# Eight trains of identity-by-ones products on TensorE, placed ahead of waits in four stages of a two-block model

## The chip, the cores and the metric

The kernel runs on one core of a Trainium2 chip. The metric is the device time of one execution in microseconds (us); lower is better. A core has five engines with instruction queues of their own, each worked through in order: TensorE (matmuls; PE in the profile), VectorE (DVE), ScalarE (ACT), GpSimd (POOL) and SyncE (SP, which here only issues transfers). Engines wait for one another by semaphores. TensorE's clock is granted by the chip at one of two levels, 1.2 and 2.4 GHz; the profile gives it as a share, 0.50 and 1.00.

## The reference

1024 tokens of width 1024 go through two blocks in float32. The first: a mixer (long convolutions and Fourier transforms), then a mixture of 32 experts in 4 groups. Each token chooses a group and two experts in it:

```python
g_sel = jnp.argmax(g_logits, axis=-1)
top_l, top_i = lax.top_k(e_logits, TOP_K)
expert = (g_sel[:, None] * EXPERTS_PER_GROUP + top_i)
...
y = (jax.nn.silu(xb @ w_gate[e]) * (xb @ w_up[e])) @ w_down[e]
```

The second block:

```python
proj = rms_norm(x) @ w_in                  # q, k, v, u, gates
mix = (g_a * y_a + g_b * y_b) @ w_o        # chunked attention and pooling, gated
x = x + rms_norm(mix)
x = x + rms_norm(conv_gated_ffn(rms_norm(x)))   # up projection to 2 x 2816, conv, gated GELU, down projection
```

## The kernel before

The stages run one after the other. Each is a block of instructions for all engines: it begins when all engines have come out of the one before, and ends when all have finished their part. Most matmuls are products of split float32 numbers, three matmuls each (`product`, lines 141 to 143). `m.ident` and `m.ones` are 128x128 float32 matrices in the on-chip memory; `keep_clock` (line 146) is defined and never called. As a measure of a plain float32 matmul: `channel_transform` (line 726) issues 32 of 128x128 by 128x128 in one train, each with weights of its own.

**The routing** (`route`, line 1379). VectorE works out from the logits which expert each token goes to, in a chain of small instructions. Twice it needs TensorE: `pairs_done` lets two matmuls go that rank the tokens (`route_ps`, lines 1446 and 1448), `rank_mm` gives them back; after `places_done` 16 matmuls build the list of rows (line 1455), `list_mm` gives it back. From the list come the row numbers (`ids_done`), and GpSimd gathers the first three blocks' rows with them (line 1375). SyncE loads the first expert weights in the meantime (line 1342) until all raw slots are full, and goes on only in the next block, `experts`, whose first work on TensorE is to transpose a block's rows (line 1644).

**The second projection's begin** (`project_second`, line 1986). For each of eight tiles of 128 tokens VectorE adds up the two expert rows and the residual and scales it twice, TensorE transposes it (line 2143, eight transposes), ScalarE and VectorE split the result into `hT`. A tile goes on when VectorE has scaled it (`scaled_done`). From tile 4 on, half a product of 24 matmuls follows the transposes. `row_done` is given once, early, when ScalarE has read a row out of the first PSUM bank.

**The end of `mix_output`** (line 2764). For each of eight tiles: 48 matmuls (`tile_product`), then the transposes of the tile before (`turn`, line 2813). The last tile's transposes stand alone, after the loop. VectorE then brings them out and mixes them with other tiles (lines 2865 to 2880), and the block ends.

**The up projection** (`ffn_up`, line 2965). ScalarE and VectorE split seven blocks of the input (`blocks_high`, `blocks_rest`) and the operands (`up_operand_high`, `up_operand_rest`). TensorE's n-th group of matmuls waits for `rest_done`.

Of the kernel before, what the change touches and what calls it, by code (L numbers as in the profile page):

```python
# [17 lines left out]
F32 = mybir.dt.float32  # L18
# [127 lines left out]
def keep_clock(nc, m, out, n):  # L146


    for _ in range(n):
        nc.tensor.matmul(out, m.ident[:], m.ones[:], start=True, stop=True)  # L150
# [1228 lines left out]
def route(nc, m, A, router, weights, rows):  # L1379
# [3 lines left out]
    with ExitStack() as mem:  # L1383
# [58 lines left out]
        @block.tensor  # L1442
        def _(pe):

            pe.wait_ge(pairs_done, 1)
            nc.tensor.matmul(ps[:, 1, 0:(TT + 1) * EXPERTS], m.ones[:], earlier[:].rearrange("p t e -> p (t e)"),
                             start=True, stop=False)
            last = nc.tensor.matmul(ps[:, 1, 0:TT * EXPERTS], before[:], both[:].rearrange("p t e -> p (t e)"),
                                    start=False, stop=True)
            last.then_inc(rank_mm, 1)  # L1450

            pe.wait_ge(places_done, 1)
            for slot in range(2):
                for t in range(TT):
                    last = nc.tensor.matmul(ps[0:CAP, 0, 0:BLOCKS], at_row[:, slot, t, :], in_block[:, slot, t, :],
                                            start=(slot == 0 and t == 0), stop=(slot == 1 and t == TT - 1))
            last.then_inc(list_mm, 1)

        @block.gpsimd
        def _(pool):  # L1460
# [511 lines left out]
def mixture(nc, m, A):  # L1972

    with ExitStack() as mem:
        m.row_ids = mem.enter_context(nc.sbuf_tensor("row_ids", [CAP, BLOCKS], I32))
        m.out_ids = mem.enter_context(nc.sbuf_tensor("out_ids", [CAP, BLOCKS], I32))
        with ExitStack() as places:
            weights = ExpertWeights(nc, m, places, A)
            weights.add_parts(nc, places)
            rows = Rows(nc, m, places)  # L1980
            with nc.psum_tensor("route_ps", [P, 2, BANK], F32) as m.router.ps:
                route(nc, m, A, m.router, weights, rows)
            experts(nc, m, A, weights, rows)


def project_second(nc, m, A, hT):
# [8 lines left out]
    with ExitStack() as mem:  # L1995
# [128 lines left out]
        @block.tensor  # L2124
        def _(pe):
            def half_product(j, half):
                n = ring_n[jobs[j]]
                cols = slice(half * BANK, (half + 1) * BANK)
                for k in range(KT):
                    last = product(nc, bank(j, half), ring.parts(n % S, k), (hT[0][:, k, cols], hT[1][:, k, cols]),  # L2130
                                   start=(k == 0), stop=(k == KT - 1))
                return last

            pe.wait_ge(cols_done, 1)
            for k in range(KT):
                last = nc.tensor.transpose(ps[:, 0, k // 4, k % 4 * P:(k % 4 + 1) * P], gamma_cols[:, k * P:(k + 1) * P], m.ident[:])
            last.then_inc(row_turned, 1)
            for t in range(TT):
                pe.wait_ge(scaled_done, t + 1)
                if t >= 2:  # L2140
                    pe.wait_ge(out_done, t - 1)
                for k in range(KT):
                    last = nc.tensor.transpose(turn_ps(t)[:, k // 4, k % 4, :], scaled[:, t % 2, k * P:(k + 1) * P], m.ident[:])
                last.then_inc(turned, 1)
                if t >= TT - EARLY:
                    j = t - (TT - EARLY)
                    if j == 0:
                        pe.wait_ge(out_done, TT // 2)
                        pe.wait_ge(row_done, 1)
                    ring.arrived(pe, j, 0)  # L2150
                    half_product(j, 0)
            pe.wait_ge(out_done, TT)
            for j in range(EARLY):
                half_product(j, 1).then_inc(ring.used[j], 1)

            for j, (kind, c) in enumerate(jobs):
                if j < EARLY:
                    continue
                pe.wait_ge(job_out, {EARLY: 2, EARLY + 1: EARLY}.get(j, j - 3))
                if kind == "g":  # L2160
                    if c == 0:
                        pe.wait_ge(small_in, 32)
                    pe.wait_ge(pooled_done, c + 1)
                    for half in range(2):
                        last = nc.tensor.matmul(ps[:, j % 4, half, :], w_g[:, c, :],
                                                pooled[:, c, half * BANK:(half + 1) * BANK], start=True, stop=True)
                    last.then_inc(job_mm, 1)
                    continue
                n = ring_n[kind, c]
                ring.arrived(pe, n % S, n // S)  # L2170
                for half in range(2):
                    last = half_product(j, half)
                last.then_inc(ring.used[n % S], 1)

            pe.wait_ge(job_out, len(jobs))
            for kk in range(KT // 2):
                n = len(tiles) + kk
                ring.arrived(pe, n % S, n // S)
                for t in range(TT):
                    here = slice(t * P, (t + 1) * P)  # L2180
                    for i in range(2):
                        k = 2 * kk + i
                        w = [part[:, n % S, 4 * i:4 * i + 4, :].rearrange("p b c -> p (b c)")
                             for part in (ring.high_part, ring.rest_part)]
                        last = product(nc, ps[:, t // 2, t % 2, :], (hT[0][:, k, here], hT[1][:, k, here]), w,
                                       start=(k == 0), stop=(k == KT - 1))
                last.then_inc(ring.used[n % S], 1)
# [576 lines left out]
def mix_output(nc, m, A, raw, blocks, up):  # L2764
# [6 lines left out]
    with ExitStack() as mem:  # L2771
# [34 lines left out]
        @block.tensor  # L2806
        def _(pe):
            def turn(t):
                pe.wait_ge(scaled_done, t + 1)
                if t >= 2:  # L2810
                    pe.wait_ge(hT_done, t - 1)
                for k in range(KT):
                    last = nc.tensor.transpose(ps_t[:, t % 2, k, :], scaled[:, t % 2, k * P:(k + 1) * P], m.ident[:])
                last.then_inc(turned, 1)

            for t in range(TT):
                wide.tile_product(pe, t, norm.left_psum, t - 1)
                if t:
                    turn(t - 1)
            turn(TT - 1)  # L2820

        @block.scalar
        def _(act):
# [141 lines left out]
def ffn_up(nc, m, A, blocks, up, pieces):  # L2965
# [8 lines left out]
    with ExitStack() as mem:  # L2974
# [61 lines left out]
        @block.sync  # L3036
        def _(sp):
            def load(f):
                sp.wait_ge(rest_done, AT[f - 2, "P4"] + 1)
                sp.wait_ge(sums_done, 4 * (f - 1))  # L3040
                up.load(sp, f)

            for f in range(FT + 1):
                if f + 2 < FT:
                    load(f + 2)
                if f:
                    sp.wait_ge(prod, f)
                    sp.dma_start(m.prod_dram[f - 1], value[:, (f - 1) % 2, :]).then_inc(stored[(f - 1) % 2], 16)
                if f == FT - 1:

                    sp.wait_ge(rest_done, len(PLAN))
                    sp.wait_ge(sums_done, 4 * FT)
                    for i in range(2):
                        sp.wait_ge(stored[i], 16 * (FT // 2 - 1))
                    for n in range(pieces.SLOTS):
                        pieces.load(sp, n)
            for i in range(2):
                sp.wait_ge(stored[i], 16 * FT // 2)
# [19 lines left out]

        @block.tensor
        def _(pe):  # L3080
            for n, (f, name) in enumerate(PLAN):
                pe.wait_ge(rest_done, n + 1)
                if n >= 8:
                    f_then, name_then = PLAN[n - 8]
                    if name_then == "P1":
                        pe.wait_ge(first_kept, f_then + 1)
                    else:
                        joined_to(pe, f_then, READ_BY[name_then])
                s, given = n % SLOTS, GIVEN[name]
                if f == 0:  # L3090
                    pe.wait_ge(blocks.rest_done, given + 1)
                for k in range(H):
                    last = product(nc, bank(f, name), (op_high[:, s, k, :], op_rest[:, s, k, :]),
                                   blocks.parts(given, k),
                                   start=(k == 0), stop=(k == H - 1))
                last.then_inc(used, 1)
# [428 lines left out]
```

## Time and profile before

| | |
|---|---|
| median of 3 runs | 2638.54 us (2632.26 to 2640.03) |
| the profiled execution | 2639.38 us, its span 2637.6 us |
| TensorE busy | 2430.7 us, 92% of the span |
| VectorE busy | 1575.9 us, 60% |
| ScalarE busy | 1063.9 us, 40% |
| mean granted clock of TensorE | 0.955 |

The page's PEclk row divides the span into slices of 1/40 (the digits are tenths of the full clock). A row of the windows view has: the stretch in us and its length, then for PE, PEld (weight loads), DVE, ACT and POOL the busy us and the number of records, then the mean granted clock, the busy share of the DMA engines and GB/s. A row of the timeline has the start in us, the duration, the engine (SPq and POOLq are queues that issue transfers), the line, the operation with output and inputs, the number of records merged, and in brackets the idle time of the engine before it and what released it.

### The profile page before, as it was taken

To read this page: it belongs to the slowest core of one execution; us is meant where nothing else is said; L and a number is where in the kernel's file an instruction comes from. 1 tells how busy PE (TensorE), PEld (TensorE's weight loads), DVE (VectorE), ACT (ScalarE), POOL (GpSimd) and SP (SyncE) were. 2 spreads that over 40 slices of the span, in tenths; PEclk is the share of its full clock that TensorE was granted. 3 is DMA by queue.
4 is the path that set the end of the run, shared out by engine and by line. 5 is a ranking of instruction groups with operands and counts; after the bars stand their busy time and mean duration, and the time that the engine had idled before them with its cause. 6 is when DMAs were issued, how large, how long until landed. Compare 5 with 4: busy or idle time off the path is not lost. (4 is left out here: it accounts for less than half of the span.)

```text
span 2637.6 us, 28239 instructions
## 1 busy us (share of the span) xinstructions
PE 2430.7 (92%) x11056; PEld 1838.1 (70%) x11056; DVE 1575.9 (60%) x1695; ACT 1063.9 (40%) x1276; POOL 420.6 (16%) x283
## 2 busy tenths in 40 slices
PE   7999988949999999975998999997969999998998
PEld 6776545836666666644776778885758888876877
DVE  5552655358999988858212652222589998873343
ACT  4221103227777776754213741112344344433332
POOL 3110300011222232320300210000032332310000
PEclk9999998959999999986999999999979999998999
DMA  4121032269999999966310011113212322225443
GB/s 157 43 69 50 20 122 82 80 237 343 384 374 377 370 376 363 374 237 230 101 48 17 2 49 48 48 48 120 80 44 78 95 80 88 80 76 212 131 156 135
DMA packets 191956, 397.25 MB, mean 151 GB/s; under 512 B 16134, under 2 KB 119686, under 8 KB 175448
## 3 DMA queue, kind: packets, MB, share of 16 engines
q1 hardware_dynamic: 182616, 378.76, 40.7%
q0 software_dynamic: 9216, 16.80, 2.1%
q8 instruction: 82, 1.34, 0.2%
q14 instruction: 42, 0.34, 0.0%
HBM read 357.75 MB, written 47.18 MB: 154 GB/s over the span
## 5 line engine op out<-in xcount | busy, mean ns | idle before, releaser
L1354 DVE TENSOR_TENSOR expert_rest<-expert_raw,expert_high 128x2048 fp32r<-128x2048 f32 x124 | 280.9, 2288 | 53.3 <-ACT expert_high L1348 41.0
L1348 ACT ACTIVATE expert_high<-expert_raw 128x2048 fp32r<-128x2048 f32 x124 | 237.4, 1914 | 54.3 <-DMA expert_raw<-in_w_up_dram 20.2
L141 PE MATMUL up_ps<-blocks_high,up_operand_high 128*128 128x512 f32 x616 | 241.6, 392 | 14.2 <-DVE up_operand_rest L3155 14.2
L143 PE MATMUL up_ps<-blocks_high,up_operand_rest 128*128 128x512 f32 x616 | 241.3, 392 | 0.0
L1734 POOL DMA_INDIRECT expert_rows<-y_rows,out_ids x32 | 102.7, 3209 | 419.5 <-DVE y_rows L1694 401.5
L1354 DVE TENSOR_TENSOR expert_rest<-res,expert_high 128x2048 fp32r<-128x2048 f32 x68 | 154.4, 2288 | 22.7 <-ACT expert_high L1348 21.9
L141 PE MATMUL down_ps<-w_down_high,prod_high 128*128 128x512 f32 x352 | 138.2, 393 | 16.1 <-DVE w_down_rest L185 16.1
L141 PEld LDWEIGHTS up_ps<-blocks_high,up_operand_high 128*128 128x128 f32 x616 | 116.7, 189 | 39.3 <-DVE up_operand_rest L3155 15.0
L3155 DVE TENSOR_TENSOR up_operand_rest<-res,up_operand_high 128x512 fp32r<-128x512 f32 x154 | 142.8, 939 | 0.2 <-ACT up_operand_high L3110 0.2
L1348 ACT ACTIVATE expert_high<-res 128x2048 fp32r<-128x2048 f32 x68 | 130.2, 1915 | 27.3 <-DMA res<-in_w_down_dram 11.0
L142 PE MATMUL up_ps<-plain_blocks_rest,up_operand_high 128*128 128x512 f32 x352 | 138.7, 394 | 0.0
L142 PE MATMUL down_ps<-w_down_rest,prod_high 128*128 128x512 f32 x352 | 137.5, 391 | 0.0
L143 PE MATMUL down_ps<-w_down_high,prod_rest 128*128 128x512 f32 x352 | 137.4, 390 | 0.0
L143 PEld LDWEIGHTS up_ps<-blocks_high,up_operand_rest 128*128 128x128 f32 x616 | 116.6, 189 | 24.5
L3068 POOL TENSOR_TENSOR res<-res 128x512 f32<-128x512 f32 x22 | 30.3, 1379 | 637.1 <-POOLq L2771 404.6
L3110 ACT ACTIVATE up_operand_high<-res 128x512 fp32r<-128x512 f32 x154 | 89.9, 622 | 83.1 <-PE up_ps L143 73.4
L141 PE MATMUL expert_gate_ps<-expert_high,x_high 128*88 128x512 f32 x256 | 103.9, 406 | 3.7 <-DVE x_rest L1680 3.7
L3334 DVE TENSOR_TENSOR prod_rest<-res,prod_high 128x512 fp32r<-128x512 f32 x44 | 30.4, 692 | 125.6 <-ACT prod_high L3320 125.6
L141 PE MATMUL y_ps<-expert_high,hid_high 128*88 128x512 f32 x256 | 102.9, 402 | 1.9 <-DVE y_rows L1694 1.9
L141 PE MATMUL gates_ps<-hT_high,gates_w_high 128*128 128x512 f32 x256 | 100.9, 394 | 3.3 <-DVE gates_w_rest L185 3.3
L142 PE MATMUL up_ps<-mixed_blocks_rest,up_operand_high 128*128 128x512 f32 x264 | 102.7, 389 | 0.0
L143 PE MATMUL expert_gate_ps<-expert_high,x_rest 128*88 128x512 f32 x256 | 102.0, 399 | 0.0
(421 smaller groups left out, 5922.9 us busy)
## 6 DMA issues: line engine op xcount, KB each, us to landing
expert_raw<-in_w_gate_dram SPq DMA_DIRECT2D x42, 1024.0 KB, 20.8
expert_raw<-in_w_down_dram SPq DMA_DIRECT2D x42, 1024.0 KB, 23.5
expert_raw<-in_w_up_dram SPq DMA_DIRECT2D x40, 1024.0 KB, 21.5
res<-in_w_up_dram SPq DMA_DIRECT2D x24, 1024.0 KB, 21.9
res<-in_w_down_dram SPq DMA_DIRECT2D x22, 1024.0 KB, 21.5
res<-in_w_gate_dram SPq DMA_DIRECT2D x22, 1024.0 KB, 25.6
res<-in_w_up_dram SPq DMA_DIRECT2D x88, 256.0 KB, 4.0
res<-in_w_down_dram SPq DMA_DIRECT2D x44, 512.0 KB, 4.1
```

The costliest lines, as they stand in the source:

```text
L141: nc.tensor.matmul(out, w_high, x_high, start=start, stop=False)
L142: nc.tensor.matmul(out, w_high, x_rest, start=False, stop=False)
L143: return nc.tensor.matmul(out, w_rest, x_high, start=False, stop=stop)
L1348: self.nc.scalar.activation(self.high_part[:, n % SPLIT_SLOTS, :], self.raw[n % RAW_SLOTS], ACT.Copy) \
L1354: self.nc.vector.tensor_tensor(self.rest_part[:, s, :], self.raw[n % RAW_SLOTS], self.high_part[:, s, :].bitcast(F32), ALU.subtract).then_ ...
L1734: pool.indirect_dma_start(m.y_dram, bass.IndirectOffsetOnAxis(ap=ids, axis=0), y[:, s, :], None, bounds_check=2 * SEQ - 1, oob_is_err=Fals ...
L3068: nc.gpsimd.tensor_tensor(sums[:, 0], a21, a22, ALU.add).then_inc(sums_done, 1)
L3110: nc.scalar.activation(op_high[:, n % SLOTS], operand(n), ACT.Copy).then_inc(high_done, 1)
L3155: nc.vector.tensor_tensor(op_rest[:, n % SLOTS], operand(n), op_high[:, n % SLOTS].bitcast(F32), ALU.subtract) \
L3334: nc.vector.tensor_tensor(x_rest[:, n % S, :], x_raw[n % S], x_high[:, n % S, :].bitcast(F32), ALU.subtract) \
```

## The change

Eight calls of `keep_clock` are added. Each issues products of the identity and the ones into a part of PSUM that nobody reads at the time: in the routing a new tile `route_clock`, elsewhere a bank whose content has been read. Nothing is removed, and a wait stands ahead of the trains in `project_second` and of the first train in `mix_output`, for the bank to be free. In all 338 products.

```diff
 # route, TensorE
+            keep_clock(nc, m, router.clock[:], 70)
             pe.wait_ge(pairs_done, 1)
...
             last.then_inc(rank_mm, 1)
 
+            keep_clock(nc, m, router.clock[:], 90)
             pe.wait_ge(places_done, 1)
...
             last.then_inc(list_mm, 1)
+            keep_clock(nc, m, router.clock[:], 40)
 # project_second, TensorE, in the loop over the tiles t
                 last.then_inc(turned, 1)
+                if t in (2, 3):
+                    pe.wait_ge(row_done, 1)
+                    keep_clock(nc, m, bank(0, 0)[:, 0:P], 24)
 # mix_output, TensorE
+            pe.wait_ge(norm.left_psum, TT - 1)
+            keep_clock(nc, m, ps[:, 0, 0, 0:P], 30)
             turn(TT - 1)
+            keep_clock(nc, m, ps[:, 0, 0, 0:P], 40)
 # ffn_up, TensorE
+            keep_clock(nc, m, ps[:, 0, 0:P], 20)
             for n, (f, name) in enumerate(PLAN):
```

The function:

```python
def keep_clock(nc, m, out, n):
    for _ in range(n):
        nc.tensor.matmul(out, m.ident[:], m.ones[:], start=True, stop=True)
```

TensorE's queue at the routing, from the logits to the first transposes of the experts, before:

```order
L1106 MATMUL logit_ps<-router_w,K 128x36 x8
L976 UNCONDITIONAL_BRANCH
L1442 UNCONDITIONAL_BRANCH
L1446 MATMUL route_ps<-earlier,ones 128x288
L1448 MATMUL route_ps<-both,before 128x256
L1455 MATMUL route_ps<-in_block,at_row 88x55 x16
L1383 UNCONDITIONAL_BRANCH
```

and with the change:

```order
L1442 UNCONDITIONAL_BRANCH
L150 MATMUL route_clock<-ones,ident 128x128 x70
L1447 MATMUL route_ps<-earlier,ones 128x288
L1449 MATMUL route_ps<-both,before 128x256
L150 MATMUL route_clock<-ones,ident 128x128 x90
L1457 MATMUL route_ps<-in_block,at_row 88x55 x16
L150 MATMUL route_clock<-ones,ident 128x128 x40
L1383 UNCONDITIONAL_BRANCH
```

Ahead of the rank products stand 70 products, ahead of the list products 90, and 40 ahead of the branch out of the block.

TensorE's queue at the second projection's begin, with the change (before, the 24, 8 and 8 transposes are one row of 40 and the rest is the same):

```order
L2139 MATMUL qkvu_ps<-ident,attT 128x128 x8
L2146 MATMUL qkvu_ps<-ident,poolT 128x128 x24
L150 MATMUL qkvu_ps<-ones,ident 128x128 x24
L2146 MATMUL qkvu_ps<-ident,poolT 128x128 x8
L150 MATMUL qkvu_ps<-ones,ident 128x128 x24
L2146 MATMUL qkvu_ps<-ident,poolT 128x128 x8
L141 MATMUL qkvu_ps<-hT_high,qkvu_w_high 128x512
```

A train of 24 now stands ahead of the transposes of tile 3 and another ahead of those of tile 4.

TensorE's queue from the last transposes of `mix_output` into the up projection, before:

```order
L143 MATMUL w_o_ps<-w_o_w_high,w_o_x_rest 128x512
L2813 MATMUL norm_ps<-ident,norm_scaled 128x128 x16
L2771 UNCONDITIONAL_BRANCH
L3079 UNCONDITIONAL_BRANCH
L141 MATMUL up_ps<-blocks_high,up_operand_high 128x512
```

and with the change:

```order
L2819 MATMUL norm_ps<-ident,norm_scaled 128x128 x8
L150 MATMUL w_o_ps<-ones,ident 128x128 x30
L2819 MATMUL norm_ps<-ident,norm_scaled 128x128 x8
L150 MATMUL w_o_ps<-ones,ident 128x128 x40
L2777 UNCONDITIONAL_BRANCH
L3088 UNCONDITIONAL_BRANCH
L150 MATMUL up_ps<-ones,ident 128x128 x20
L141 MATMUL up_ps<-blocks_high,up_operand_high 128x512
```

The train of 30 stands between the last two tiles' transposes, the 40 ahead of the block's end, the 20 at the next block's head.

## Rows read from the trace of the kernel before

**Rows 1.** The page's header and its row of TensorE's clock
```profile
span 2637.6 us, 28239 instructions
...
PEclk9999998959999999986999999999979999998999
```

**Rows 2.** Windows over the routing, the expert stage's end, and the other stretches
```profile
546.00:590.00 44.00, 8.80 (x45) 7.36 (x46) 28.56 (x74) 11.17 (x9) 7.05 (x5) 0.50 0.81 306
...
1006.00:1146.00 140.00, 133.84 (x627) 89.36 (x626) 119.81 (x76) 101.17 (x77) 38.79 (x13) 1.00 1.00 364
...
1196.00:1226.00 30.00, 9.90 (x41) 8.30 (x42) 29.06 (x33) 17.75 (x34) 0.00 (x0) 0.50 0.62 250
...
1924.00:1946.00 22.00, 3.44 (x18) 2.71 (x17) 16.22 (x18) 9.98 (x13) 7.04 (x4) 0.57 0.06 24
```

**Rows 3.** Timeline of the routing and of the next block's begin, all engines
```profile
545.98 0.18 DVE L1497 TENSOR_REDUCE gmax<-logits 128x8 f32<-128x32 f32 x1 [1.44 <-PEq L3439]
...
555.27 1.33 PE L1446 MATMUL route_ps<-earlier,ones 128*128 128x288 f32 x2 [11.23 <-DVE earlier L1525]
...
557.56 0.46 DVE L1539 COPY rank<-route_ps 128x288 f32<-128x288 f32 x1 [1.21 <-PE route_ps L1448]
...
569.76 4.94 PE L1455 MATMUL route_ps<-in_block,at_row 128*88 128x55 f32 x32 [12.31 <-DVE in_block L1577]
...
574.74 0.21 DVE L1592 TENSOR_SCALAR second_slot<-route_ps 88x55 f32<-88x55 f32 x1 [0.50 <-PE route_ps L1455]
...
579.20 1.07 POOL L1375 DMA_INDIRECT rows<-normed_rows,row_ids  x1 [0.30 <-issue]
...
585.61 0.34 SPq L1342 DMA_DIRECT2D expert_raw<-in_w_gate_dram  x1
...
586.55 1.43 PE L1644 MATMUL x_ps<-ident,rows 88*128 88x88 f32 x8 [11.85 <-PEq L1383]
```

**Rows 4.** Timeline of TensorE, fp32 matmuls of 128x128 in a train
```profile
301.75 7.31 PE L726 MATMUL mix_ps<-pair,folded 128*128 128x128 f32 x64
...
308.89 0.95 PE L793 MATMUL mix_ps<-mixT,pair 128*128 128x1 f32 x8
```

**Rows 5.** Timeline of the second projection's begin, TensorE and VectorE
```profile
1209.97 1.97 PE L2143 MATMUL qkvu_ps<-ident,poolT 128*128 128x128 f32 x8 [5.60 <-DVE poolT L2311]
...
1217.54 1.97 PE L2143 MATMUL qkvu_ps<-ident,poolT 128*128 128x128 f32 x8 [5.60 <-DVE poolT L2311]
...
1223.97 1.97 PE L2143 MATMUL qkvu_ps<-ident,poolT 128*128 128x128 f32 x8 [4.47 <-DVE poolT L2311]
...
1227.72 0.39 PE L143 MATMUL qkvu_ps<-hT_high,qkvu_w_rest 128*128 128x512 f32 x1
...
1229.07 1.28 DVE L2311 SCALAR_TENSOR_TENSOR poolT<-res,norm_stats,attT 128x1024 f32<-128x1024 f32 x1
...
1232.08 1.03 PE L2143 MATMUL qkvu_ps<-ident,poolT 128*128 128x128 f32 x8
```

**Rows 6.** Timeline from the end of `mix_output` into the up projection
```profile
1923.82 1.03 PE L2813 MATMUL norm_ps<-ident,norm_scaled 128*128 128x128 f32 x8
...
1931.04 1.97 PE L2813 MATMUL norm_ps<-ident,norm_scaled 128*128 128x128 f32 x8 [6.19 <-DVE norm_scaled L2858]
...
1937.88 0.69 DVE L2880 TENSOR_TENSOR mixT<-mixT,mixed_blocks 128x512 f32<-128x512 f32 x1
...
1938.87 1.91 ACT L2937 ACTIVATE blocks_high<-mixT 128x2048 fp32r<-128x2048 f32 x1 [9.13 <-PEq L2771]
...
1945.38 0.79 PE L141 MATMUL up_ps<-blocks_high,up_operand_high 128*128 128x512 f32 x1 [12.37 <-DVE up_operand_rest L3155]
...
1951.09 0.42 PE L142 MATMUL up_ps<-plain_blocks_rest,up_operand_high 128*128 128x512 f32 x1
...
1963.75 0.50 PE L141 MATMUL up_ps<-blocks_high,up_operand_high 128*128 128x512 f32 x1 [1.80 <-DVE up_operand_rest L3155]
```

More of the change, by code:

```diff
@@ L1980, in mixture @@
             rows = Rows(nc, m, places)
-            with nc.psum_tensor("route_ps", [P, 2, BANK], F32) as m.router.ps:
+            with nc.psum_tensor("route_ps", [P, 2, BANK], F32) as m.router.ps, nc.psum_tensor("route_clock", [P, P], F32) as m.router.clock:
                 route(nc, m, A, m.router, weights, rows)
```

## The prediction

> **What bounds the kernel now.** I read first the page's header and clock row, then windows over the stretches in which TensorE waits, then the timeline of each of them.
>
> The page's clock row is at 9 nearly everywhere and falls in a few slices [rows 1]. The windows show why: in the routing (546 to 590 us) TensorE is busy 8.80 of 44 us at a granted clock of 0.50, at the second projection's begin 9.90 of 30 us at 0.50, around the up projection's begin 3.44 of 22 us at 0.57 [rows 2]. 0.50 is the lower of the two levels (1.2 GHz), 1.00 the upper (2.4 GHz). What runs there at 0.50 is little, so the clock itself can give back only a few us. What bounds these stretches is a chain through VectorE, and the reader is to see its stations in the routing [rows 3]: VectorE starts at 545.98; the rank products start at 555.27, released by `earlier`; VectorE takes their sum at 557.56; the list products start at 569.76, released by `in_block`; VectorE takes the list at 574.74; GpSimd's third gather is issued at 579.20, SyncE's first load of the next block at 585.61, TensorE's first transposes of the experts at 586.55. TensorE's own free time in it is 545.98 to 555.27 (9.3 us) and some 12 us ahead of the list. Any work put ahead of a wait on TensorE is free only as far as it ends by then, since its queue is in order.
>
> **The price of one product.** No `keep_clock` product is in the trace of before. The nearest row has the same form, 128x128 fp32 on 128x128 weights, each with a weight load: 64 records from 301.75 to the next row's start at 308.89 [rows 4]. The code that issues them makes 32 matmuls, so an fp32 matmul is two records, and one costs 7.14 / 32 = 0.223 us at clock 1.00. At 0.50 eight transposes take 1.97 us and at 1.00 1.03 us [rows 6], a ratio of 1.91, so there a product is some 0.44 us.
>
> How soon the clock rises once the engine is dense: at 1223.97 transposes and then matmuls follow each other, and the matmuls shorten from 1227.72 on, some 3.5 us later [rows 5]; at 1945.38 it takes until 1951.09, 5.7 us [rows 6]. I take 3.5 and keep 5.7 as the other end.
>
> The Trainium skill has a smaller figure. Its page "TensorE: Matmul & The Clock Gate", section "Back-to-back issue gap", gives about 56 ns for 128 columns at the full clock, and 81 ns in a stream of weight load and matmul. By it the 70 products would be over after some 6 to 8 us, ahead of the rank products, and the routing would lose nothing. The row of this kernel is 223 ns for the fp32 form, and I go by the row; the page's smaller price is the mechanism of the first rival.
>
> **The change part by part.**
>
> *Routing, 70 products.* They start with the block at 545.98. In 3.5 us at 0.50 go 8 products, the other 62 take 13.8 us: end at 563.3. The rank products were due at 555.27, so they are 8.0 us late. They now run at 1.00: VectorE got their sum 2.29 us after their start, now some 1.2 us after it, at 564.5.
>
> *90 products.* They start when the rank products are issued, about 564.35, and take 20.1 us: end at 584.4. VectorE's chain from the sum to the list's inputs is 569.76 - 557.56 = 12.2 us and would be ready at 576.7. The list is 7.7 us late again. It took 4.98 us to VectorE's read (569.76 to 574.74), at 1.00 some 2.5: read at 586.9 instead of 574.74, **12.2 us late**. With 5.7 us to the rise it is 13.3. What is queued behind: VectorE has nothing else in these waits, ScalarE's and SyncE's work of the block is long done, and GpSimd waits for the ids; so gathers, the block's end and the next block's loads all move by 12.2.
>
> *40 products.* From 586.8, 8.9 us: end at 595.8. The block's end was at about 585.6, when SyncE goes on, and is now 597.8; so these are covered, by the gathers, with 2.0 us over. TensorE then idles some 3 us until the transposes at 598.7. If the clock is still 1.00 then, the transposes save 0.7 us and the first matmuls 1.4; if it has fallen, nothing. Idle times of 6.2 us ended at 0.50 (the 1931.04 row), none of 3 us with known history is among the rows. I take -0.5 (0 to -2.1). The expert stage itself has its DMA engines full and TensorE waiting 6 of 140 us late in it [rows 2], so a gain at its begin may be lost there; the delay is not, since the loads start only at 585.61.
>
> *Second projection, 24 after the transposes of tiles 2 and 3.* `row_done` is long given, that wait costs nothing. Tile 2: dense from 1209.97, at 1.00 from 1213.5; the transposes are out at 1211.75, then 4 products at 0.50 and 20 at 1.00: end 1217.95. Tile 3's transposes were due at 1217.54 [rows 5], so 0.4 late, but at 1.00 they end 0.6 before they did. Then 24 at 1.00, 5.4 us: 1224.2 against tile 4 at 1223.97. Its transposes and the 24 matmuls behind them (0.23 us each, from 1227.72 to 1232.08 for 19) end at 1230.55, where before it was 1232.08; tile 5 is ready at 1229.07 + 1.28 = 1230.35. That is a gain of 1.5 us. VectorE is busy 29.06 of 30 us here [rows 2] and can take part of it back: I take **-1.2** (-0.5 with the slow rise; 0 if VectorE takes all).
>
> *End of `mix_output`.* The wait for `left_psum` is already met. 30 products follow the transposes of 1923.82 (0.87 us to issue): 1924.7 + 6.7 = 1931.4 at 1.00; the last transposes were due at 1931.04 but now run in 1.03 instead of 1.97, so VectorE, which comes to them later than both (its last `mixT` mixing starts at 1937.88), sees nothing. Then 40 products, 1932.3 + 8.9 = 1941.2. The block ended with VectorE at 1938.57 and ScalarE began the next at 1938.87 [rows 6]. Now TensorE is last: with its end at 1941.3 and the same 0.3 us, the next block starts at 1941.65, **2.8 us late**.
>
> *Up projection, 20 products.* 1941.65 + 4.5 = 1946.1, ahead of the first matmul, now 1945.38 + 2.8 = 1948.2: covered. Thirteen matmuls ran there at 0.50 before 1951.09, worth 13 x 0.2 = 2.6 us of TensorE's time, but at 1963.75 TensorE waits for VectorE's `up_operand_rest` again [rows 6]; what it gains before that it only waits longer. Value 0 (bounds -1 to +1, as the clock behind that wait may be better or worse).
>
> **Sum**: 12.2 - 0.5 - 1.2 + 2.8 + 0 = +13.3 us. Against the profiled execution's 2639.38 us (its span is 2637.6) that is 2652.7; the median of the runs is 0.84 lower, so **2652 us**, +0.5%. About 0.3% (8 us) is what a measurement of this kernel can tell from no change.
>
> **The rivals.**
>
> *A, the products are cheap (6%).* A product costs about half of the row's price, one record of 0.11 us. It decides below 9.3 / 70 = 0.133 us a product, the slow first ones counted in. Then all trains end inside their waits: 8 x 0.2 us of slow rank and list products, 1.1 + 2.5 us, are saved, 1.0 at the experts, 1.2 at the projection, and the 40 at `mix_output`'s end are over by 1936.7: 2639.4 - 5.8, so 2633 us, not slower. For it: eight transposes of 128 columns run in 1.03, 0.13 each [rows 6]. Against it: a transpose is one record, an fp32 product two [rows 4].
>
> *B, identity and ones do not lift the clock (3%).* Then all of the routing's trains go at 0.44: the 70 end at 576.8, the 90 at 618.7, the list is 49 us late, and the 40 end at 641, behind the block's end: +56; at the projection tile 4 waits for two trains of 10.6, +11; some +20 at `mix_output` and the up projection, whose 30, 40 and 20 take 13.2, 17.6 and 8.8: 2726 us. Against it: the fp32 row of the same form runs 7.3 us at its fast pace without falling.
>
> *C, TensorE holds up the block's end in the routing (4%).* The step from the list to 585.61 might be TensorE's own, 11 us after its last product, not the gathers'. Then the 40 products add their 8.9 us: 2661 us. Against it: SyncE goes on 5.3 us after the third gather ended.
>
> *D, the routing's delay is swallowed (3%).* If the expert stage ended with a stream of loads that didn't care when it began, only +2.8 - 1.2 would be left: 2641 us. Against it: the loads' next issue is itself at 585.61.
>
> **How the numbers follow.** The main case has 84%. Its own ends: 12.0 - 2.1 - 1.5 + 2.8 = +11 and 13.3 + 2.8 + 1 = +17, so 2650 to 2656. The range takes in C and the spread of the runs of before, down to 2645 and up to 2661; A and B stay out. Slower by over 0.3%: main, B and C, 0.91, less 0.01 for a main case that falls short. Within 0.3%: D and most of A, 0.07. Faster: 0.03 for A with more given back.
>
> **What would show it.** In the profile after: the 70 products end near 563, the rank products start behind them without idle time; the 90 end near 584, and VectorE waits some 22 us for the list products; SyncE's next loads at about 598. The clock is 1.00 over most of the routing. At 1224 + 12 tile 4's transposes follow their train directly. `blocks_high` begins 2.8 us later than the shift up to there. It would be wrong if a product costs under 0.133 us, if the clock stays at 0.50 in the trains, or if something in the expert stage gives back more than 5 us.

## The result, and the profile after

With the change the kernel takes 2649.34 us (median of 6 runs, 2644.52 to 2655.62) against 2638.03 us before (6 runs): a ratio of 1.0048, 95% interval 1.0036 to 1.0061, so 9.5 to 16.1 us slower. The forecast was 2652, slower. TensorE's mean granted clock rose from 0.955 to 0.97 and its busy time from 2430.7 to 2497.5 us. Two executions among the experiments below, one of e8's twelve (2855.55 us) and one of the kernel before beside it (9237.75 us), lie far outside the others and are left out of the ratios.

The page's header, busy row and clock row of the changed kernel:

```profile
span 2647.7 us, 29591 instructions
...
PE 2497.5 (94%) x11732; PEld 1908.7 (72%) x11732; DVE 1577.9 (60%) x1695; ACT 1065.0 (40%) x1276; POOL 406.6 (15%) x283
...
PEclk9999998989999999997999999999999999998999
```

The digits that were lowest in the middle [rows 1] have risen (5 to 8 in the slice with the routing, 8 to 9 and 6 to 7 around the second projection's begin, 7 to 9 around the up projection's): the trains do lift the clock. The timeline of the routing shows what that cost, station by station against [rows 3]:

```profile
545.72 0.19 DVE L1500 TENSOR_REDUCE gmax<-logits 128x8 f32<-128x32 f32 x1 [1.44 <-PEq L3449]
545.72 18.72 PE L150 MATMUL route_clock<-ones,ident 128*128 128x128 f32 x140 [1.94 <-PEq L3449]
564.27 0.65 PE L1447 MATMUL route_ps<-earlier,ones 128*128 128x288 f32 x2
565.19 20.26 PE L150 MATMUL route_clock<-ones,ident 128*128 128x128 f32 x180
...
565.46 0.46 DVE L1542 COPY rank<-route_ps 128x288 f32<-128x288 f32 x1 [9.37 <-PE route_ps L1449]
...
576.54 1.07 DVE L1580 TENSOR_TENSOR in_block<-in_block,place 128x880 f32<-128x880 f32 x1
...
585.29 2.64 PE L1457 MATMUL route_ps<-in_block,at_row 128*88 128x55 f32 x32
587.77 9.16 PE L150 MATMUL route_clock<-ones,ident 128*128 128x128 f32 x80
587.97 0.21 DVE L1595 TENSOR_SCALAR second_slot<-route_ps 88x55 f32<-88x55 f32 x1 [5.82 <-PE route_ps L1457]
...
598.69 0.34 SPq L1342 DMA_DIRECT2D expert_raw<-in_w_gate_dram  x1
599.63 1.43 PE L1647 MATMUL x_ps<-ident,rows 88*128 88x88 f32 x8 [2.71 <-PEq L1383]
```

The block begins 0.26 us earlier than before. The 70 products (140 records) take 18.55 us, where the wait they stand in was 9.3. VectorE gets the ranks 1.19 us after the rank products start (2.29 before). The 90 products end 20.1 us after their start, at 585.29, while `in_block` was ready at 576.54 + 1.07 = 577.6. The list goes to VectorE after 2.68 us instead of 4.98. The last train of 40 is over before the block's end, TensorE still idles 2.71 us. SyncE's next load comes 13.08 us later than before, 13.34 against the block's begin.

Windows of the changed kernel, columns as before: the first train's slow part, the rest of the routing, the experts' begin, and the two other stretches of [rows 2], here 10 us later because the stages are:

```profile
546.00:552.00 6.00, 6.00 (x31) 6.00 (x31) 4.97 (x22) 1.30 (x3) 2.33 (x1) 0.53 0.91 328
552.00:600.00 48.00, 45.29 (x411) 44.95 (x410) 20.30 (x50) 7.58 (x5) 3.40 (x3) 0.99 0.58 220
600.00:606.00 6.00, 4.23 (x16) 2.81 (x15) 6.00 (x4) 2.56 (x2) 1.06 (x1) 0.50 0.90 314
1206.00:1236.00 30.00, 19.93 (x139) 19.05 (x140) 29.06 (x33) 18.21 (x34) 0.00 (x0) 0.70 0.63 249
1934.00:1956.00 22.00, 19.90 (x173) 19.46 (x173) 14.97 (x17) 8.68 (x10) 7.15 (x4) 1.00 0.06 25
```

The clock stayed at 0.50 for nearly 6 us of products before it rose, and fell again in the 2.71 us of idle time ahead of the experts, whose first matmuls ran at 0.50 as before.

The other two places, timeline of the changed kernel, against [rows 5] and [rows 6]:

```profile
1221.77 6.65 PE L150 MATMUL qkvu_ps<-ones,ident 128*128 128x128 f32 x48
1228.26 1.04 PE L2146 MATMUL qkvu_ps<-ident,poolT 128*128 128x128 f32 x8
1229.13 5.52 PE L150 MATMUL qkvu_ps<-ones,ident 128*128 128x128 f32 x48
1234.49 1.04 PE L2146 MATMUL qkvu_ps<-ident,poolT 128*128 128x128 f32 x8
...
1938.52 1.04 PE L2819 MATMUL norm_ps<-ident,norm_scaled 128*128 128x128 f32 x8
1939.39 9.10 PE L150 MATMUL w_o_ps<-ones,ident 128*128 128x128 f32 x80
...
1945.01 0.69 DVE L2889 TENSOR_TENSOR mixT<-mixT,mixed_blocks 128x512 f32<-128x512 f32 x1
...
1948.77 1.91 ACT L2946 ACTIVATE blocks_high<-mixT 128x2048 fp32r<-128x2048 f32 x1 [11.89 <-PEq L2777]
1948.79 4.70 PE L150 MATMUL up_ps<-ones,ident 128*128 128x128 f32 x40 [0.30 <-PEq L2777]
...
1955.29 0.50 PE L141 MATMUL up_ps<-blocks_high,up_operand_high 128*128 128x512 f32 x1 [1.80 <-DVE up_operand_rest L3165]
1959.19 0.50 PE L141 MATMUL up_ps<-blocks_high,up_operand_high 128*128 128x512 f32 x1 [0.89 <-DVE up_operand_rest L3165]
```

At the end of `mix_output` VectorE is done at 1945.70, and the next block begins only at 1948.77, when the 40 products are over. The up projection's first matmul runs at 1.00 now, but its second group waits for VectorE.

### The profile page after: what moved, and what is told of

It reads as the page before. It is cut to its first block and busy times, and to the rows that moved or that the text cites. A ratio compares the mean times of both kernels' runs of the same rounds, so it can differ in the third digit from the quotient of the medians.

```text
span 2647.7 us, 29591 instructions
## 1 busy us (share of the span) xinstructions
PE 2497.5 (94%) x11732; PEld 1908.7 (72%) x11732; DVE 1577.9 (60%) x1695; ACT 1065.0 (40%) x1276; POOL 406.6 (15%) x283
## 5 line engine op out<-in xcount | busy, mean ns | idle before, releaser
L1348 ACT ACTIVATE expert_high<-expert_raw 128x2048 fp32r<-128x2048 f32 x124 | 237.3, 1914 | 44.3 <-DMA expert_raw<-in_w_up_dram 13.5
L141 PE MATMUL down_ps<-w_down_high,prod_high 128*128 128x512 f32 x352 | 138.2, 393 | 16.1 <-DVE w_down_rest L185 16.1
L1737 POOL DMA_INDIRECT expert_rows<-y_rows,out_ids x32 | 83.6, 2614 | 429.3 <-DVE y_rows L1697 414.9
L142 PE MATMUL expert_gate_ps<-expert_rest,x_high 128*88 128x512 f32 x256 | 102.2, 399 | 0.0
```

The costliest lines, as they stand in the source:

```text
L141: nc.tensor.matmul(out, w_high, x_high, start=start, stop=False)
L142: nc.tensor.matmul(out, w_high, x_rest, start=False, stop=False)
L1348: self.nc.scalar.activation(self.high_part[:, n % SPLIT_SLOTS, :], self.raw[n % RAW_SLOTS], ACT.Copy) \
L1737: pool.indirect_dma_start(m.y_dram, bass.IndirectOffsetOnAxis(ap=ids, axis=0), y[:, s, :], None, bounds_check=2 * SEQ - 1, oob_is_err=Fals ...
```

## The experiments

Four kernels and then four more were run, each set beside the kernel before on one chip. Differences in us are the ratio times before's median there (2635).

**e1: the routing's trains alone.** The lines of the change outside `route` are taken out again:

```diff
-                if t in (2, 3):
-                    pe.wait_ge(row_done, 1)
-                    keep_clock(nc, m, bank(0, 0)[:, 0:P], 24)
...
-            keep_clock(nc, m, ps[:, 0, 0, 0:P], 30)
...
-            keep_clock(nc, m, ps[:, 0, 0, 0:P], 40)
...
-            keep_clock(nc, m, ps[:, 0, 0:P], 20)
```

> The change's three trains of the routing alone (70, 90, 40). Theory 1 (the routing's delay passes whole into the time): SyncE's first load of the expert block starts 13 us later than before, and the time is 12 to 13 us above before. Theory 2 (the expert stage gives back some 4 us whenever it begins late, as it did in the profile of the change): the load starts 13 us later too, the expert stage is 3 to 4 us shorter than before's 592 us, and the time is 8.5 to 9.5 us above before.

Measured: ratio 1.0055 (1.0041 to 1.0069), +14.5 us (10.8 to 18.2). The experts' first transposes begin 53.69 us after the routing's first instruction, before 40.57: 13.1 us later. The interval takes in theory 1's 12 to 13 us and leaves theory 2's 8.5 to 9.5 out.

**e2: the change without the routing's trains.**

```diff
-            keep_clock(nc, m, router.clock[:], 70)
...
-            keep_clock(nc, m, router.clock[:], 90)
...
-            keep_clock(nc, m, router.clock[:], 40)
```

> The change without the routing's three trains: 24 and 24 at the second projection, 30 and 40 at the end of mix_output, 20 in the up projection. Both theories: the routing as before; blocks_high begins 2.8 us later against the end of mix_output's matmuls, the second projection gives back 0.5 to 1.2 us: +1.5 to +2.5 us against before in sum. Theory 2's rival, that something after the projection's begin gives back more (1.6 us between 1250 and 1420 us in the change's profile), would show as 0 to +0.7 us.

Measured: 0.9999 (0.9991 to 1.0008), -0.3 us (-2.4 to +2.1). The loss is all the routing's. The +1.5 to +2.5 us expected here did not come, because the stages behind the second projection's begin and the up projection give back more than was counted (the table of stages below).

**e3: the trains fitted to their waits.** Three are shortened, two are lengthened, and there are 255 products instead of 338:

```diff
-            keep_clock(nc, m, router.clock[:], 70)
+            keep_clock(nc, m, router.clock[:], 27)
...
-            keep_clock(nc, m, router.clock[:], 90)
+            keep_clock(nc, m, router.clock[:], 52)
...
-            keep_clock(nc, m, router.clock[:], 40)
+            keep_clock(nc, m, router.clock[:], 46)
...
-            keep_clock(nc, m, ps[:, 0, 0, 0:P], 40)
+            keep_clock(nc, m, ps[:, 0, 0, 0:P], 25)
...
-            keep_clock(nc, m, ps[:, 0, 0:P], 20)
+            keep_clock(nc, m, ps[:, 0, 0:P], 27)
```

> All eight trains, five of them with another count so that each ends inside its wait: 27 (for 70), 52 (90), 46 (40) in the routing, 25 (for 40) at the end of mix_output, 27 (for 20) in the up projection. If what cost time was the overrun and nothing else, the rank products start with the same delay behind earlier as before (within 0.3 us), rank and list products save 1.1 and 2.4 us, the experts' first transposes and matmuls 1 to 2 us, the second projection 0.5 to 1.2: 5 to 7 us below before, 2631 to 2633. If the trains cost something by themselves (queue, instruction loading), it stays within 3 us of before.

Measured: 0.9982 (0.9973 to 0.9990), -4.7 us (-7.1 to -2.6). The sign turns with the numbers of products alone. Timeline of e3's routing, the list products and VectorE:

```profile
546.24 9.19 PE L150 MATMUL route_clock<-ones,ident 128*128 128x128 f32 x54 [1.94 <-PEq L3449]
555.54 0.75 PE L1447 MATMUL route_ps<-earlier,ones 128*128 128x288 f32 x2
...
569.04 2.71 PE L1457 MATMUL route_ps<-in_block,at_row 128*88 128x55 f32 x32 [0.70 <-DVE in_block L1580]
...
571.24 2.27 DVE L1354 TENSOR_TENSOR expert_rest<-expert_raw,expert_high 128x2048 fp32r<-128x2048 f32 x1
...
573.45 0.20 DVE L1595 TENSOR_SCALAR second_slot<-route_ps 88x55 f32<-88x55 f32 x1
...
584.67 0.83 PE L1647 MATMUL x_ps<-ident,rows 88*128 88x88 f32 x8 [2.58 <-PEq L1383]
587.83 0.73 PE L141 MATMUL expert_gate_ps<-expert_high,x_high 128*88 128x512 f32 x1 [2.33 <-DVE x_rest L1683]
```

The rank products start 9.30 us after the block's begin, as in before (9.29). The list products take 2.71 us instead of 4.94, but VectorE reads them 4.41 us after their start (4.98 before): it has a 2.27 us split of expert weights (line 1354) in between. So 0.6 us comes out where 2.4 were expected. The transposes behind the wait of 2.58 us are still fast (0.83 us for eight, against 1.43 in the change), but at 587.83, behind the next wait of 2.33 us, the experts' matmuls are slow again (0.73 us).

**e4: the same lateness, no products.** In the kernel before, VectorE repeats one step of its chain eight times:

```diff
+            for _ in range(8):
+                step(nc.vector.tensor_tensor(at_row[:].rearrange("p s t c -> p (s t) c"),
+                                             r_of[:].rearrange("p s t -> p (s t)").unsqueeze(2).to_broadcast(pairs + [CAP]),
+                                             router.count[:].unsqueeze(1).to_broadcast(pairs + [CAP]), ALU.is_equal))
```

> The kernel before, no products; VectorE repeats one step of its chain in the routing (the comparison that fills at_row, 1.6 us) eight times more, so that everything behind is some 13 us late while TensorE idles at its low clock. Theory 1: the time is 13 us above before, the expert stage as long as before. Theory 2, where a late begin alone makes the expert stage shorter: it is 3 to 4 us shorter, the time 9 us above. Should e1 give back 4 us and this one nothing, it is the warm or busy TensorE that does it.

Measured: 1.0058 (1.0044 to 1.0072), +15.3 us (11.6 to 19.0), with the experts 13.5 us later (54.03 against 40.57). The same lateness from an idle TensorE costs the same. Theory 2 fell: the expert stage is 588.27 us here, but it is 588.2 to 589.4 us as well in the four kernels whose routing and experts are those of before and begin on time (e2, e5, e6, e8); so the 591.67 of before's profile is that execution's own; its cause stays open.

**e5: the second projection's two trains alone**; **e6: those of `mix_output` and the up projection alone.** Each is the change with the other lines taken out, as in e1.

> The change's two trains of 24 at the second projection's begin alone. By the stages of the profiles so far: the second projection's begin 1.2 us shorter. The idle time of 2.1 us some 120 us later (at 1370 in the profile of before) was followed by matmuls at 0.50 in the three profiles without these trains and at 1.00 in the three with them. If the trains do that, another 1.6 us are saved here, the stage up to the first score products is as long as with the change, and the time is 2.8 us below before; if it was chance, 1.2 us below, and the matmuls behind that idle time may be at 0.50.

> The change's trains at the end of mix_output (30, 40) and in the up projection (20) alone. From the end of mix_output's matmuls to blocks_high 2.1 to 2.9 us longer than before, from there to the first down matmul 0 to 1.1 us shorter: +1 to +2.9 us against before. The idle time of 2.1 us near 1370 is followed by matmuls at 0.50 if the second projection's trains decide it.

Measured: e5 0.9987 (0.9978 to 0.9996), -3.4 us (-5.8 to -1.1); e6 1.0011 (1.0002 to 1.0020), +2.9 us (+0.5 to +5.3). The idle time near 1367, timeline of TensorE in e5 and then in e6:

```profile
1367.16 0.50 PE L141 MATMUL qkvu_ps<-qkvu_w_high,hT_high 128*128 128x512 f32 x1 [2.14 <-ACT mixT L2251]
...
1368.88 0.39 PE L142 MATMUL qkvu_ps<-qkvu_w_rest,hT_high 128*128 128x512 f32 x1
1369.11 0.39 PE L143 MATMUL qkvu_ps<-qkvu_w_high,hT_rest 128*128 128x512 f32 x1
```

```profile
1368.22 0.50 PE L141 MATMUL qkvu_ps<-qkvu_w_high,hT_high 128*128 128x512 f32 x1 [2.14 <-ACT mixT L2248]
...
1369.60 0.63 PE L143 MATMUL qkvu_ps<-qkvu_w_high,hT_rest 128*128 128x512 f32 x1
1370.03 0.63 PE L141 MATMUL qkvu_ps<-qkvu_w_high,hT_high 128*128 128x512 f32 x1
```

After the same wait of 2.14 us the matmuls stay at 0.39 us in e5 and go to 0.63 in e6.

**e7: more trains where TensorE waits; e8: two of them alone.** e7 is e3 with these, and 53 for 46; e8 is the kernel before with the last two:

```diff
 # experts, behind the first block's transposes
             turn(0)
+            keep_clock(nc, m, ps_y[:, 0, 0:P], 9)
...
 # ffn_up, behind the last group
+            pe.wait_ge(first_kept, FT)
+            keep_clock(nc, m, bank(FT - 1, "P1")[:, 0:P], 44)
...
 # ffn_down, ahead of the first
+            keep_clock(nc, m, ps[:, 0, 0, 0:P], 12)
```

> As e3 (all trains fitted into their waits), with 53 for 46 behind the list products, 9 more between the experts' first transposes and their first matmul, 44 at the end of ffn_up and 12 at the begin of ffn_down. If a train that is over in time gives back what the slow matmuls behind the wait cost: 13 matmuls at the experts' begin (2.6 us) and 7 at ffn_down's begin (1.4 us) on top of e3's -4.7: 8 to 9 us below before, 2627 or less. If VectorE or the transfers are what sets these begins, it stays at e3's time.

> The kernel before with the two trains at the border of ffn_up and ffn_down alone (44 and 12). The first matmuls of ffn_down at 1.00 and not at 0.50: seven of them are 0.2 us shorter each, 1.4 us below before; no change if VectorE's w_down_rest paces them.

Measured: e7 0.9975 (0.9964 to 0.9985), -6.6 us (-9.5 to -4.0), an interval that overlaps e3's and also holds the 8 to 9 us expected if the fast matmuls count; e8 1.0000 (0.9990 to 1.0010), 2.6 us either way, which holds its expected 1.4 as well. So the times decide nothing here, and only the stages of the profiles can. The clock did what was asked at all three places. Timeline of TensorE in e7, at the experts' and at `ffn_down`'s begin:

```profile
586.58 2.21 PE L150 MATMUL y_ps<-ones,ident 128*128 128x128 f32 x18
589.08 0.47 PE L141 MATMUL expert_gate_ps<-expert_high,x_high 128*88 128x512 f32 x1 [0.29 <-DVE x_rest L1683]
589.39 0.40 PE L142 MATMUL expert_gate_ps<-expert_rest,x_high 128*88 128x512 f32 x1
...
2369.01 2.92 PE L150 MATMUL down_ps<-ones,ident 128*128 128x128 f32 x24 [1.04 <-PEq L2984]
2371.88 0.50 PE L141 MATMUL down_ps<-w_down_high,prod_high 128*128 128x512 f32 x1
2372.22 0.39 PE L142 MATMUL down_ps<-w_down_rest,prod_high 128*128 128x512 f32 x1
```

At the experts it is fast from the first matmul on, and yet the expert stage lasts 587.39 us against e3's 587.23: nothing of it comes out.

At the down projection some of it does. The stage has a later wait of 1.97 us in every profile. It ends 123.16 us behind the first down matmul in e8 and 123.99 before, 123.42 in e7 and 124.47 in e3: the fast begin has put TensorE 0.8 and 1.0 us ahead. In e8 this lasts to the end of the kernel (251.99 us from the first down matmul, 252.87 before). In e7 it does not (253.88 against e3's 253.30), because behind that wait the matmuls run at 0.50 for some 3 us, in this profile alone. Timeline of TensorE in e7 and then in e8:

```profile
2495.30 0.50 PE L141 MATMUL down_ps<-w_down_high,prod_high 128*128 128x512 f32 x1 [1.97 <-DVE w_down_rest L185]
...
2496.03 0.63 PE L143 MATMUL down_ps<-w_down_high,prod_rest 128*128 128x512 f32 x1
```

```profile
2504.24 0.50 PE L141 MATMUL down_ps<-w_down_high,prod_high 128*128 128x512 f32 x1 [1.97 <-DVE w_down_rest L185]
...
2504.80 0.39 PE L143 MATMUL down_ps<-w_down_high,prod_rest 128*128 128x512 f32 x1
```

Each of these is one profile, and 0.8 us is below what the ratio of e8 can tell from nothing.

**The stages side by side**, each the difference of two starts in the run's profile: routing from `gmax` to the experts' transposes; experts to the second projection's first VectorE copy; from there to the memset behind tile 8 (second); to the first score products (qkv); from w_o's first matmul to `blocks_high` (mix); to the first down matmul (up).

| | routing | experts | second | qkv | mix | up |
|---|---|---|---|---|---|---|
| before | 40.57 | 591.67 | 69.87 | 172.80 | 127.77 | 445.85 |
| after | 53.91 | 587.82 | 69.39 | 171.21 | 130.69 | 445.82 |
| e1 routing only | 53.69 | 588.31 | 70.51 | 172.80 | 127.53 | 442.13 |
| e2 without routing | 40.07 | 589.42 | 68.79 | 171.16 | 129.84 | 441.05 |
| e3 fitted | 38.43 | 587.23 | 68.94 | 171.17 | 127.47 | 441.04 |
| e4 late list | 54.03 | 588.27 | 70.36 | 172.77 | 127.58 | 442.16 |
| e5 second only | 40.62 | 589.15 | 68.47 | 171.16 | 128.03 | 441.62 |
| e6 mix and up only | 40.09 | 588.55 | 70.27 | 172.79 | 130.59 | 441.03 |
| e7 more trains | 38.61 | 587.39 | 68.70 | 171.16 | 127.39 | 441.04 |
| e8 down only | 40.03 | 588.17 | 70.20 | 172.79 | 128.03 | 445.83 |

(Up in e7 and e8 is taken to the first down matmul behind the train, 2371.88 and 2381.08.)

## Why the prediction was right

**The price of a product** was the step that decided, and it held: 20.1 us for 90 at 1.00 is 0.223 each. Rival A, half that price, is refuted by the same train.

**The 70 products** ended 18.55 us after the block's begin. The prediction had 17.3 with 3.5 us to the rise and 18.4 with 5.7; the slow end of that bound was right. The routing cost 13.34 us in the profile, where the sum had 12.2 and its slow end 13.3.

**What passed on.** Rivals C and D are out: from VectorE's read of the list to SyncE's next load it is 10.72 us with the 40 products in between and 10.87 before without them, and e4 shows the lateness paid in full. Rival B is out by the windows at 0.99.

**"VectorE has nothing else in these waits"** was wrong. It has the split of line 1354 behind the list's inputs. That did not matter with the trains as long as they are, since it was over long before the list came (at 582.14, against 587.97); it is what makes the list's faster products nearly worthless in e3.

**VectorE's wait for the list** was to be some 22 us as a sign of being right. That reading was off: of the 22.5 us between its two reads (565.46 and 587.97) VectorE is at work on its chain and that split until 582.14, and its idle time is the 5.82 us of the row. Rival A has a slip too: its "8 x 0.2 us" is not the 1.1 + 2.5 us that it goes on with. Neither enters the forecast.

**The experts' begin** was put at -0.5 and is worth nothing: the clock fell again, and e7 shows that keeping it up would not have helped.

**The second projection** was put at -1.2. Its stage is 68.5 to 69.4 us in the five profiles with its trains and 69.9 to 70.5 in the five without, means 68.86 and 70.24, so 1.4. What was missed are another 1.6 us in the qkv stage: 171.2 in all five with the trains, 172.8 in all five without. Together 3.0 of e5's 3.4.

**The end of `mix_output`** was put at +2.8: 130.69 against 127.77 in the change, +2.9.

**The up projection** was put at 0. The pair before and after has 445.85 and 445.82. In the other profiles the stage is 441.0 to 441.1 with the 20 products and 441.6 to 442.2 without, some 1 us, leaving aside e8, which like that pair has some 4 us more. These 4 us are not the trains', since they come with and without them. Timeline of GpSimd and VectorE before, and then in e1 at the same place of the stage:

```profile
1955.00 3.17 POOL L3068 TENSOR_TENSOR res<-res 128x512 f32<-128x512 f32 x1 [8.53 <-DVE up_operand_rest L3155]
...
1956.95 1.77 DVE L3155 TENSOR_TENSOR up_operand_rest<-res,up_operand_high 128x512 fp32r<-128x512 f32 x1
...
1958.65 3.38 DVE L2941 TENSOR_TENSOR plain_blocks_rest<-mixT,blocks_high 128x2048 fp32r<-128x2048 f32 x1
```

```profile
1966.52 10.59 POOL L3071 TENSOR_TENSOR res<-res 128x512 f32<-128x512 f32 x1 [8.54 <-DVE up_operand_rest L3158]
...
1968.46 0.68 DVE L3158 TENSOR_TENSOR up_operand_rest<-res,up_operand_high 128x512 fp32r<-128x512 f32 x1
1969.06 2.28 DVE L2944 TENSOR_TENSOR plain_blocks_rest<-mixT,blocks_high 128x2048 fp32r<-128x2048 f32 x1
```

Before, in the change and in e8 GpSimd's step takes 3.17 us and VectorE's beside it 1.77 and 3.38; in the seven other profiles GpSimd's takes 10.59 us and VectorE's 0.68 and 2.28. Where VectorE is the slow one, its next operand is 2.2 us later, TensorE waits for it (1.80 us before [rows 6], 1.95 in the change), and the next eight matmuls or so run at 0.50. The seven have no wait there. Against e1, before's 1.8 us of wait and some 0.2 us for each of the eight slow matmuls make 3.4 of the 3.7 us between their stages. From this place to its last matmul of the stage TensorE has no wait of 0.3 us in any of the ten profiles, so the stage keeps what was lost. Why the two engines meet in one way or the other was not found out. The prediction's reason for the 0, that TensorE only waits longer for VectorE, holds in the change (waits of 0.89, 0.88 and 1.95 us behind the first) and fails in the profiles without that last wait, where 1 us comes out.

By the terms as measured, 13.3 - 1.4 - 1.6 + 2.9 - 1 is +12.2 us, and +13.2 without the last term, as in the pair; both are inside the interval of 9.5 to 16.1. That the two profiles differ by only 10.1 us of span is before's own long expert stage, 591.67 where the nine others have 587.2 to 589.4.

The mechanism was the forecast one, products that outlast their waits, and it carries 13.3 of these us. That the total came so near to the forecast +13.3 is in part luck: the routing was 1.1 us too low and the experts' begin 0.5 too favourable, while the 1.6 us of the qkv stage and up to 1 us of the up projection were missed.

## What to carry to other kernels

A filler train on an in-order engine is free only up to the end of its wait: count products times the duration of the same instruction form in the trace (an fp32 matmul is two records here), the slow ones before the clock rises counted in, and compare with the wait. The same eight trains were a loss of 9.5 to 16.1 us with 338 products and a gain of 2.6 to 7.1 us with 255, fitted to their waits (e3). And look first at who sets the stage behind the wait: at the experts a fast begin gave nothing (e7), while in the up and down projections, where TensorE hardly waits afterwards, about 1 us of it stayed in the profiles.

## What the runs showed of the hardware that was not expected

The rise of the clock took nearly 6 us of products without a gap in the routing (0.53 over 546 to 552), close to the 5.7 us seen at the up projection before and longer than the 3.5 us at the second projection.

An idle time of 2.14 us near 1370 us was followed by matmuls at 0.50 in all five profiles without the second projection's trains, and at 1.00 in all five with them, though TensorE worked at 1.00 for some 140 us or more in between in both, with no gap over 0.5 us. It is worth 1.6 us. Why trains so far back decide it was not found out. The traces leave one rival that no run tests: the moment. With the trains the clock rises earlier in the second projection, and the wait begins 152.6 to 153.3 us behind that rise; without them it begins 139.9 to 140.4 us behind it (before: the rise at 1227.5, the wait from 1367.92). The wait of the down projection shows that length alone does not decide: the same 1.97 us at the same place ended at 0.50 in e7 and at 1.00 in the nine other profiles.

Elsewhere, idle times of 2.71 us (the change) and of 2.33 us (e3), ahead of the experts, ended at 0.50, and one of 2.58 us (e3) just before that at 1.00.
